# Level scores of two branches in three groups of two on TensorE, with VectorE's order changed to match

## The chip, the cores and the metric

One core of a Trainium2 chip runs the whole kernel. The metric is device time in microseconds, the median of the runs. PE is TensorE, DVE is VectorE, ACT is ScalarE, POOL is GpSimd, SP is SyncE, whose queue brings in the weights.

## The reference, cut to what matters

A decoder trunk of two layers: 512 tokens, width 1024. Each layer has a mixer of four parallel branches (mLSTM, GLA, S5, HGRN2), a cross-attention and an MLP. The change touches the two branches that use this function (GLA with 4 heads of 32 keys, HGRN with 4 heads of 64), in chunks of 64 tokens:

```python
def step(s_st, inp):
    qb, kb, vb, gb = inp
    g_end = gb[:, :, -1, :]
    o_inter = jnp.einsum('bhtk,bhkv->bhtv', qb * jnp.exp(gb), s_st)
    diff = gb[:, :, :, None, :] - gb[:, :, None, :, :]
    decay = jnp.exp(jnp.where(causal[:, :, None], diff, -jnp.inf))
    att = jnp.einsum('bhtk,bhsk,bhtsk->bhts', qb, kb, decay)
    o = o_inter + jnp.einsum('bhts,bhsv->bhtv', att, vb)
    s_new = (jnp.exp(g_end)[..., None] * s_st
             + jnp.einsum('bhsk,bhsv->bhkv', kb * jnp.exp(g_end[:, :, None, :] - gb), vb))
    return s_new, o
```

The branch outputs are normalised, gated, projected by `w_branch`, multiplied by sigmoid gates of the input (`gate` columns of `w_in`), summed, and projected by `w_out`.

## The kernel before

**Every engine has a list of its own, written out by hand.** Each runs its list in order; semaphores tie them. A wait at the head of an engine's list holds back all that stands behind it.

**Big matmuls.** Each weight matrix comes in blocks of 256 columns. A block (`gemm("m_o")`, `gate_parts(3, 1)`, `branch_gemm(3, 0)`) is cut into units of 256 rows: SP loads a unit, ACT writes its rounded part (`feed`, L1391), POOL the remainder, and PE does 12 matmuls of 128x128 by 512 for a unit (three products of split numbers, `parts`). A block of full depth has 4 units, a branch block 1. `some(block, n)` runs n units of a block and `rest(block)` what is left, so that other work can be put between. Blocks use two pairs of PSUM banks by turns; a block can start when the one before the last has been read out: of a gate block by ACT's tanh, of a branch block by DVE's `merge(n, c)` (L1982), which multiplies it by the gate and adds it up.

**Levels.** Within a chunk, the scores are split into seven levels: level 0 is the diagonal, and level l = 1 to 6 holds pairs of blocks of 32, 16, 8, 4, 2 and 1 tokens. For a branch m (`hg` or `gl`) and a level l:
- DVE `level_diff(m, l)` (L2002) writes the differences of the log decays to `m.E[l % 2]`; for l of 3 or more it needs level_mul l - 2.
- ACT `level_exp(m, l)` (L1510) takes the exponential in place.
- DVE `level_mul(m, l)` (L2014) multiplies keys and queries by it, into buffers that also go by l % 2; it needs the exponential, and for l of 3 or more that PE has done the scores of l - 2. It raises `x_ready`.
- PE `scores(m, l)` (L825, `pair_scores` L804): 32 small matmuls into the `mix` banks, when level_mul l is done and the bank is free. For HGRN, level l needs pick l - 4; for GLA, pick l - 2.
- DVE `pick(m, l)` (L2032) copies the valid scores from the bank into the score matrix under a mask.

Then DVE `last_decay` and `decayed` (L2056, L2063) make the decayed keys, with ACT's exponentials (`decays`, L1514) between them; PE `decayed_keys` (L853) transposes them, for which `decayed` and the picks that read the same banks must be done (HGRN pick 4, GLA pick 5); ACT copies them out; PE `state_in` (L862) needs pick 6 as well; DVE `states` adds up the chunk states and PE does `outputs`.

**ACT's list in the GLA part** is: exponential of level 1, copies of `m_v` (when PE has done that block), exponential of level 2 (L1676), copies of `m_o`, exponentials of levels 3 to 6, gate 3_1, `decays(gl)`, three tanhs for the mLSTM convolution, gate 3_2. The change leaves ACT's list as it is.

**Before the change** PE does the scores of levels 1 to 6 one by one, with 24 (HGRN) or 36 (GLA) big matmuls between two levels, and DVE picks each level as it comes.

Of the kernel before, what the change touches and what calls it, by code (L numbers as in the profile page):

```python
# [209 lines left out]
def build(nc, ins, out):  # L210
# [7 lines left out]
    with ctx:  # L218
# [59 lines left out]
        def of_layer(s, count):  # L278
            return s, count + now[0] * PER_LAYER[s.name]
# [211 lines left out]
        block = ctx.enter_context(nc.Block())  # L491
# [189 lines left out]
        def _(pe):  # L681
# [98 lines left out]
            def some(block, n):  # L780
                for _ in range(n):
                    next(block)

            def rest(block):
                for _ in block:
                    pass
# [38 lines left out]
            def scores(m, l):  # L825

                if l == 0:
                    pe.wait_ge(*of_layer(m.kq_ready, 3 - m.J))
                    if m.J == 2:
                        pe.wait_ge(*of_layer(m.g_ready, 5))  # L830
                    else:
                        pe.wait_ge(*of_layer(head_rs, 4))
                else:
                    pe.wait_ge(*of_layer(m.x_ready, l))
                if l >= 1:
                    pair_scores(m, l)
                    return
                kk, qq = (m.K, m.Q) if l == 0 else (m.X[l % 2], m.X[l % 2])

                n = CH if l == 0 else CH // 2  # L840
                for h in range(4):
                    rows = slice(m.dk * (h % m.per), m.dk * (h % m.per) + m.dk)
                    base = (h // m.per) * SEQ
                    for c in range(NCH):
                        at_ = m.score_cols(h) + (c // 2) * CH
                        tok = slice(base + c * CH, base + c * CH + CH)
                        late = qq[rows, tok]
                        if l:
                            late = late.rearrange("p (n a c) -> p n a c", a=2, c=LEVELS[l])[:, :, 1, :]
                        i = mm(m.score_bank(l, h)[64 * (c % 2):64 * (c % 2) + 64, at_:at_ + n], kk[rows, tok], late)  # L850
                i.then_inc(m.lev_done, 1)
# [104 lines left out]
            for L in range(DEPTH):  # L956
# [42 lines left out]
                    pe.wait_ge(p_vec, 10)  # L999
                mm(M[2][:, :], WA2[:, :], NT).then_inc(narrow_pe, 1)  # L1000
                rest(block)
                pe.wait_ge(*of_layer(gl.gate_in, 2))
                scores(hg, 1)
                block = parts("r_g", *H)
                some(block, 2)
                scores(hg, 2)
                rest(block)
                scores(hg, 3)
                block = gate_parts(3, 0)
                some(block, 2)  # L1010
                scores(hg, 4)
                rest(block)
                scores(hg, 5)
                block = parts("m_q", *H)
                some(block, 2)
                scores(hg, 6)
                some(block, 1)
                decayed_keys(hg)
# [9 lines left out]
                some(block, 1)  # L1028
                scores(gl, 0)
                rest(block)  # L1030
                scores(gl, 1)
                block = parts("m_o", *H)
                some(block, 3)
                scores(gl, 2)
                rest(block)
                branch_gemm(3, 0)
                scores(gl, 3)
                block = gate_parts(3, 1)
                some(block, 3)
                scores(gl, 4)  # L1040
                rest(block)
                branch_gemm(3, 1)
                block = gate_parts(3, 2)
                some(block, 1)
                scores(gl, 5)
                rest(block)
                scores(gl, 6)
                branch_gemm(3, 2)
                block = gate_parts(3, 3)
# [882 lines left out]
        def _(dve):  # L1932
# [81 lines left out]
            def level_mul(m, l):  # L2014
                w = LEVELS[l]
                dve.wait_ge(*of_layer(m.e_ready, l))
                if l >= 3:
                    dve.wait_ge(*of_layer(m.lev_done, l - 1))
                v = lambda ap: ap.rearrange("p (n a c) -> p n a c", a=2, c=w)
                e, xx, k, q = v(m.E[l % 2]), v(m.X[l % 2]), v(m.K), v(m.Q)  # L2020
                keys = KEYS[m.J][l % 2]
                if l <= (1, 2)[m.J - 1]:
                    tt(keys, m.E[l % 2], m.K, ALU.mult)
                else:
                    tt(v(keys)[:, :, 0, :], e[:, :, 0, :], k[:, :, 0, :], ALU.mult)
                of_chunk = lambda ap: ap.rearrange("p (n s) c -> p n s c", s=CH // (2 * w))
                late = m.X[l % 2].rearrange("p (n h s c) -> p n h s c", h=2, s=CH // (2 * w), c=w)
                for h in range(2):
                    own = const("in_pair")[:, 2 * m.J - 2 + h:2 * m.J - 1 + h]
                    stt(late[:, :, h, :, :], of_chunk(e[:, :, 1, :]), own, of_chunk(q[:, :, 1, :]), ALU.mult, ALU.mult, m.x_ready if h else None)  # L2030
# [96 lines left out]
            for L in range(DEPTH):  # L2127
# [71 lines left out]
                dve.wait_ge(*of_layer(gl.gate_in, 3))  # L2199
                stt(R(30)[:, 0, :], R(30)[:, 0, :], 0.0, R(31)[:, 0, :], ALU.min, ALU.subtract)  # L2200
                do(dve.tensor_tensor_scan(gl.Gc, reset, R(30)[:, 0, :], 0.0, ALU.mult, ALU.add))
                pick(hg, 1)
                level_diff(hg, 4)
                gate_out("g_r", gl.GR)
                level_mul(hg, 3)
                pick(hg, 2)
                level_diff(hg, 5)
                level_mul(hg, 4)
                pick(hg, 3)
                level_diff(hg, 6)  # L2210
                gate_out("r_g", hg.GR)
                level_mul(hg, 5)
                pick(hg, 4)
                level_mul(hg, 6)
                last_decay(hg)
                pick(hg, 5)
                decayed(hg)
                pick(hg, 6)
                decayed_queries(hg)
                states(hg)  # L2220
# [34 lines left out]
                do(dve.memset(CIN[:, :, 0:3], 0.0))  # L2255
                do(dve.memset(MONES, 1.0))
                level_mul(gl, 1)
                pick(gl, 0)
                level_diff(gl, 3)
                pick(gl, 1)  # L2260
                do(dve.tensor_copy(pr(17), Ur[:, S5_T, :]))
                do(dve.tensor_copy(pr(18), Ui[:, S5_T, :]))
                tt(Ur[:, :, :], Ur[:, :, :], PS[:, 8:8 + S5_T + 1, :], ALU.mult)
                tt(Ui[:, :, :], Ui[:, :, :], PS[:, 8:8 + S5_T + 1, :], ALU.mult)
                level_mul(gl, 2)
                level_diff(gl, 4)
                pick(gl, 2)
                tt(pr(5), re_, re_, ALU.mult)
                tt(pr(6), im_, im_, ALU.mult)
                tt(pr(5), pr(5), pr(6), ALU.add)  # L2270
# [9 lines left out]
                tt(pr(19), pr(19), pr(5), ALU.mult)  # L2280
                level_mul(gl, 3)
                level_mul(gl, 4)
                level_diff(gl, 5)
                level_diff(gl, 6)
                pick(gl, 3)
                merge(3, 0)
                conv(0)
                conv(1)
                pick(gl, 4)
                level_mul(gl, 5)  # L2290
                level_mul(gl, 6)

                def silu_of(j):
                    dve.wait_ge(*of_layer(ms["mth_ready"], j + 1))
# [1 line left out]

                last_decay(gl)
                conv(2)
                pick(gl, 5)
                decayed(gl)  # L2300
                merge(3, 1)
                conv(3)
                silu_of(0)
                silu_of(1)
                pick(gl, 6)
                decayed_queries(gl)
                merge(3, 2)
# [476 lines left out]
```

## Time and profile before

| what | us |
|---|---|
| median of 3 runs | 1968.84 (1968.78 to 1968.87) |
| the profiled execution | 1968.68 |
| its span, first to last instruction | 1966.8 |
| PE busy | 1936.9 (98%) |
| DVE busy | 1252.5 (64%) |
| POOL busy | 1134.1 (58%) |
| ACT busy | 966.5 (49%) |
| mean granted TensorE clock | 0.998 |

How to read it: the profile is of one execution. A row of the timeline gives the start and the length of a run of like instructions, the engine, the line, the operation, what is written and read with its shape, the count, and in brackets the idle time before it with what ended it. Most DVE rows carry the lines of two helpers (L1935, L1944), so they are told apart by shape, order and time. Times in the tables are from the start of the span. Layer 0's HGRN levels run from 93 to 130 us and its GLA levels from 157 to 214; layer 1's are 966 us later.

### The profile page before, as it was taken

How to read it: one execution, taken by the hardware profiler on the slowest of the kernel's cores; microseconds unless marked ns; L12 is line 12 of the kernel's file. 1: busy time of each engine (PE TensorE's matmuls, PEld its weight loads, DVE VectorE, ACT ScalarE, POOL GpSimd, SP SyncE). 2: the span in 40 equal slices, each digit the busy share in tenths (PEclk: the TensorE clock that was granted, in tenths of full speed). 3: DMA queues.
4: the chain of work that ended last, by engine and by line, in shares of the span. 5: the costliest groups of instructions: out<-in, count | busy, mean ns of one | idle time of the engine just before them, and what ended most of it. 6: DMA issues, size and time to landing. Idle time of an engine off the chain costs nothing.

```text
span 1966.8 us, 33324 instructions
## 1 busy us (share of the span) xinstructions
PE 1936.9 (98%) x12723; PEld 1642.3 (84%) x12723; DVE 1252.5 (64%) x1914; ACT 966.5 (49%) x1664; POOL 1134.1 (58%) x1356
## 2 busy tenths in 40 slices
PE   7999999999999999999999999999999999999998
PEld 6788788888888788989887877888898878989887
DVE  5887778856145766667358787787631566676662
ACT  6754545345445644344455546353553555444334
POOL 5565554946834556656564555368585446556653
PEclk9999999999999999999999999999999999999999
DMA  6423333333422333333333233233343233333331
GB/s 184 114 76 82 82 83 89 86 108 108 145 88 79 90 101 102 101 99 99 100 98 81 71 86 82 76 90 87 114 139 111 71 91 97 103 97 102 97 102 70
DMA packets 197275, 190.89 MB, mean 97 GB/s; under 512 B 23738, under 2 KB 190204, under 8 KB 196732
## 3 DMA queue, kind: packets, MB, share of 16 engines
q1 hardware_dynamic: 196252, 186.66, 32.5%
q8 instruction: 101, 1.65, 0.3%
q10 hardware_dynamic: 864, 2.10, 0.3%
q14 instruction: 58, 0.48, 0.1%
HBM read 184.51 MB, written 3.15 MB: 95 GB/s over the span
## 4 chain that ended last, share of the span: by engine, by line
PE 89%; DVE 6%; ACT 3%; issue 1%; DMA 1%; DVEq 0%; POOL 0%; SPq 0%; ACTq 0%
PE gemm L683 69%; PE mix L683 18%; DVE work L1935 1%; DVE h_lo L1944 1%; ACT w_hi L1401 1%; DVE sums_raw L1935 1%; DVE work_split L1944 1%; DVE x_t L1935 0%; DMA w_raw<-in_mlp_w_dram 0%; DVE work L1944 0%; PE mix L1265 0%; DMA work<-in_norm_mix_dram 0%; DVE gate_t L1944 0%; DVE w_raw L1935 0%; ACT work_split L1569 0%
## 5 line engine op out<-in xcount | busy, mean ns | idle before, releaser
L676 POOL TENSOR_TENSOR w_lo<-w_raw,w_hi 128x256 fp32r<-128x256 f32 x676 | 590.8, 874 | 804.6 <-ACT w_hi L1401 804.6
L677 POOL TENSOR_TENSOR w_lo<-w_raw,w_hi 128x256 fp32r<-128x256 f32 x676 | 594.6, 880 | 0.0
L683 PE MATMUL gemm<-h_hi,w_hi 128*128 128x512 f32 x1312 | 519.4, 396 | 3.6 <-DVE h_lo L1944 2.1
L683 PE MATMUL gemm<-h_lo,w_hi 128*128 128x512 f32 x1312 | 511.2, 390 | 0.0
L683 PE MATMUL gemm<-h_hi,w_lo 128*128 128x512 f32 x1312 | 511.1, 390 | 0.0
L683 PE MATMUL gemm<-work_split,w_hi 128*128 128x512 f32 (+1 forms) x1552 | 447.4, 373 | 2.7 <-ACTq L1507 1.4
L1401 ACT ACTIVATE w_hi<-w_raw 128x512 fp32r<-128x512 f32 x676 | 378.2, 621 | 53.3 <-DMA w_raw<-in_w_in_dram 24.7
L683 PEld LDWEIGHTS gemm<-work_split,w_hi 128*128 128x128 f32 x1552 | 281.2, 188 | 54.4 <-DVE work_split L1944 2.6
L683 PEld LDWEIGHTS gemm<-h_hi,w_hi 128*128 128x128 f32 x1312 | 246.3, 188 | 64.7 <-issue 8.8
L683 PEld LDWEIGHTS gemm<-h_hi,w_lo 128*128 128x128 f32 x1312 | 246.3, 188 | 52.0
L683 PE MATMUL gemm<-work_split,w_lo 128*128 128x512 f32 (+1 forms) x776 | 288.5, 372 | 0.0
L683 PEld LDWEIGHTS gemm<-h_lo,w_hi 128*128 128x128 f32 x1312 | 246.4, 188 | 49.7 <-issue 1.0
L683 PEld LDWEIGHTS gemm<-work_split,w_lo 128*128 128x128 f32 x776 | 146.2, 188 | 25.5
L1935 DVE TENSOR_TENSOR x_t<-x_t,gemm 128x512 f32<-128x512 f32 x96 | 66.0, 688 | 119.8 <-PE gemm L683 114.7
L1399 ACT ACTIVATE gate_rows<-sums_raw 128x768 fp32r<-128x768 f32 x48 | 40.6, 846 | 201.8 <-DVE sums_raw L1935 201.8
L1935 DVE TENSOR_TENSOR work<-work 128x512 f32<-128x512 f32 (+5 forms) x142 | 125.0, 880 | 14.3 <-ACT work L1612 6.5
L683 PE MATMUL mix<-work_split,w_hi 128*128 128x256 f32 (+1 forms) x544 | 121.0, 286 | 0.1
L1506 ACT ACTIVATE gate_t<-gemm 128x512 f32<-128x512 f32 x52 | 31.1, 599 | 141.0 <-PE gemm L683 140.5
L683 PE MATMUL mix<-work_split,gate_rows 128*128 128x256 f32 x456 | 97.8, 283 | 0.0
L683 PEld LDWEIGHTS mix<-work_split,w_hi 128*128 128x128 f32 x544 | 91.9, 191 | 3.2 <-issue 0.8
L683 PEld LDWEIGHTS mix<-work 64*64 64x64 f32 (+4 forms) x3136 | 76.9, 129 | 17.7 <-issue 14.4
L1935 DVE TENSOR_TENSOR sums_raw<-w_raw 128x256 f32<-128x256 f32 (+1 forms) x53 | 31.9, 601 | 84.5 <-DMA w_raw<-in_mlp_w_dram 83.2
(363 smaller groups left out, 2742.1 us busy)
## 6 DMA issues: line engine op xcount, KB each, us to landing
w_raw<-in_mlp_w_dram SPq DMA_DIRECT2D x256, 256.0 KB, 2.7
w_raw<-in_w_in_dram SPq DMA_DIRECT2D x208, 256.0 KB, 2.7
w_raw<-in_xattn_w_kv_dram SPq DMA_DIRECT2D x64, 256.0 KB, 3.0
w_raw<-in_w_branch_dram SPq DMA_DIRECT2D x32, 256.0 KB, 2.7
w_raw<-in_w_out_dram SPq DMA_DIRECT2D x32, 256.0 KB, 2.7
w_raw<-in_xattn_w_q_dram SPq DMA_DIRECT2D x32, 256.0 KB, 2.8
w_raw<-in_xattn_w_o_dram SPq DMA_DIRECT2D x32, 256.0 KB, 2.7
w_raw<-in_w_in_dram SPq DMA_DIRECT2D x32, 128.0 KB, 3.4
```

The costliest lines, as they stand in the source:

```text
L676: pool.tensor_tensor(lo[:, 0:half], raw[:, 0:half], hi[:, 0:half].bitcast(F32), ALU.subtract)
L677: pool.tensor_tensor(lo[:, half:], raw[:, half:], hi[:, half:].bitcast(F32), ALU.subtract).then_inc(split_ready, 1)
L683: return pe.matmul(o, w, a, start=start, stop=stop, skip_group_check=True)
L1399: act.activation(SWhi[d // 2 % 2], SWraw[d // 2 % 2], ACT.Copy)
L1401: act.activation(hi, raw, ACT.Copy).then_inc(split_hi, 1)
L1506: do(act.activation(t[:, b, :], G[s][b][:, :], ACT.Tanh, scale=0.5), th_ready)
L1935: do(dve.tensor_tensor(o, a, b, op), s)
L1944: do(dve.scalar_tensor_tensor(out=o, in0=a, scalar=sc, in1=b, op0=op0, op1=op1), s)
```

## The change

On PE, the scores of levels 1 and 2, 3 and 4, 5 and 6 now stand side by side, for both branches, and the parts of big blocks that stood between them come before the pair. On DVE, the two `level_mul` of a pair are done one after the other, and then the two picks. In the GLA part `level_mul(gl, 2)` comes ahead of `pick(gl, 0)`; picks 1 and 2 go behind `level_mul(gl, 4)`; `decayed(gl)` and `pick(gl, 5)` go behind `merge(3, 1)` and `conv(3)`, and `pick(gl, 5)` also behind two `silu_of`. Nothing is added to or taken from any engine's list; what is computed is the same.

```diff
@@ -999,20 +999,20 @@
                     pe.wait_ge(p_vec, 10)
                 mm(M[2][:, :], WA2[:, :], NT).then_inc(narrow_pe, 1)
                 rest(block)
+                block = parts("r_g", *H)
+                some(block, 2)
                 pe.wait_ge(*of_layer(gl.gate_in, 2))
                 scores(hg, 1)
-                block = parts("r_g", *H)
-                some(block, 2)
                 scores(hg, 2)
                 rest(block)
-                scores(hg, 3)
                 block = gate_parts(3, 0)
                 some(block, 2)
+                scores(hg, 3)
                 scores(hg, 4)
                 rest(block)
-                scores(hg, 5)
                 block = parts("m_q", *H)
                 some(block, 2)
+                scores(hg, 5)
                 scores(hg, 6)
                 some(block, 1)
                 decayed_keys(hg)
@@ -1028,22 +1028,21 @@
                 some(block, 1)
                 scores(gl, 0)
                 rest(block)
-                scores(gl, 1)
                 block = parts("m_o", *H)
                 some(block, 3)
+                scores(gl, 1)
                 scores(gl, 2)
                 rest(block)
                 branch_gemm(3, 0)
-                scores(gl, 3)
                 block = gate_parts(3, 1)
                 some(block, 3)
+                scores(gl, 3)
                 scores(gl, 4)
                 rest(block)
                 branch_gemm(3, 1)
                 block = gate_parts(3, 2)
-                some(block, 1)
+                rest(block)
                 scores(gl, 5)
-                rest(block)
                 scores(gl, 6)
                 branch_gemm(3, 2)
                 block = gate_parts(3, 3)
@@ -2199,22 +2198,22 @@
                 dve.wait_ge(*of_layer(gl.gate_in, 3))
                 stt(R(30)[:, 0, :], R(30)[:, 0, :], 0.0, R(31)[:, 0, :], ALU.min, ALU.subtract)
                 do(dve.tensor_tensor_scan(gl.Gc, reset, R(30)[:, 0, :], 0.0, ALU.mult, ALU.add))
-                pick(hg, 1)
                 level_diff(hg, 4)
                 gate_out("g_r", gl.GR)
                 level_mul(hg, 3)
+                level_mul(hg, 4)
+                pick(hg, 1)
                 pick(hg, 2)
                 level_diff(hg, 5)
-                level_mul(hg, 4)
-                pick(hg, 3)
                 level_diff(hg, 6)
                 gate_out("r_g", hg.GR)
                 level_mul(hg, 5)
+                level_mul(hg, 6)
+                pick(hg, 3)
                 pick(hg, 4)
-                level_mul(hg, 6)
                 last_decay(hg)
+                decayed(hg)
                 pick(hg, 5)
-                decayed(hg)
                 pick(hg, 6)
                 decayed_queries(hg)
                 states(hg)
@@ -2255,16 +2254,14 @@
                 do(dve.memset(CIN[:, :, 0:3], 0.0))
                 do(dve.memset(MONES, 1.0))
                 level_mul(gl, 1)
+                level_mul(gl, 2)
                 pick(gl, 0)
                 level_diff(gl, 3)
-                pick(gl, 1)
+                level_diff(gl, 4)
                 do(dve.tensor_copy(pr(17), Ur[:, S5_T, :]))
                 do(dve.tensor_copy(pr(18), Ui[:, S5_T, :]))
                 tt(Ur[:, :, :], Ur[:, :, :], PS[:, 8:8 + S5_T + 1, :], ALU.mult)
                 tt(Ui[:, :, :], Ui[:, :, :], PS[:, 8:8 + S5_T + 1, :], ALU.mult)
-                level_mul(gl, 2)
-                level_diff(gl, 4)
-                pick(gl, 2)
                 tt(pr(5), re_, re_, ALU.mult)
                 tt(pr(6), im_, im_, ALU.mult)
                 tt(pr(5), pr(5), pr(6), ALU.add)
@@ -2280,15 +2277,17 @@
                 tt(pr(19), pr(19), pr(5), ALU.mult)
                 level_mul(gl, 3)
                 level_mul(gl, 4)
+                pick(gl, 1)
+                pick(gl, 2)
                 level_diff(gl, 5)
                 level_diff(gl, 6)
-                pick(gl, 3)
                 merge(3, 0)
                 conv(0)
                 conv(1)
-                pick(gl, 4)
                 level_mul(gl, 5)
                 level_mul(gl, 6)
+                pick(gl, 3)
+                pick(gl, 4)
 
                 def silu_of(j):
                     dve.wait_ge(*of_layer(ms["mth_ready"], j + 1))
@@ -2296,12 +2295,12 @@
 
                 last_decay(gl)
                 conv(2)
-                pick(gl, 5)
-                decayed(gl)
                 merge(3, 1)
                 conv(3)
+                decayed(gl)
                 silu_of(0)
                 silu_of(1)
+                pick(gl, 5)
                 pick(gl, 6)
                 decayed_queries(gl)
                 merge(3, 2)
```

## Rows read from the trace of the kernel before

**Rows 1.** The page: busy time by engine, and the chain's shares by engine.
```profile
PE 1936.9 (98%) x12723; PEld 1642.3 (84%) x12723; DVE 1252.5 (64%) x1914; ACT 966.5 (49%) x1664; POOL 1134.1 (58%) x1356
...
PE 89%; DVE 6%; ACT 3%; issue 1%; DMA 1%; DVEq 0%; POOL 0%; SPq 0%; ACTq 0%
```

**Rows 2.** The chain in order of time: start us, us, what.
```profile
1939.92 13.38 PE gemm L683 x59
```

**Rows 3.** Timeline of PE, HGRN levels 1 and 2 of layer 0.
```profile
92.90 1.15 PE L683 MATMUL mix<-work 128*64 128x64 f32 x32
...
99.65 1.15 PE L683 MATMUL mix<-work 128*64 128x64 f32 x32
```

**Rows 4.** Groups of PE by form: count | busy us, mean ns of one | idle.
```profile
L683 PE MATMUL mix<-work 128*64 128x64 f32 x384 | 13.8, 225 | 0.0
```

**Rows 5.** Timeline of PE: GLA levels 1 to 3, transposes, state_in.
```profile
164.32 0.69 PE L683 MATMUL mix<-work 64*64 64x64 f32 x32
...
173.33 0.69 PE L683 MATMUL mix<-work 64*64 64x64 f32 x32
...
179.97 0.69 PE L683 MATMUL mix<-work 64*64 64x64 f32 x32 [0.28 <-DVE work L1944]
...
210.54 0.60 PE L859 MATMUL mix<-consts_sb,work 128*128 128x128 f32 x4
...
214.06 1.42 PE L683 MATMUL mix<-work 64*32 64x64 f32 x64
```

**Rows 6.** Timeline of PE, HGRN outputs of layer 0.
```profile
141.48 2.79 PE L683 MATMUL mix<-work 64*64 64x64 f32 x120
```

**Rows 7.** Timeline of ACT: m_v's last copy, exponentials 2 and 3 of GLA.
```profile
164.43 0.60 ACT L1674 ACTIVATE work<-gemm 128x512 f32<-128x512 f32 x1 [0.84 <-PE gemm L683]
165.14 0.63 ACT L1512 ACTIVATE work<-work 128x512 f32<-128x512 f32 x1
...
177.73 1.30 ACT L1512 ACTIVATE work<-work 128x512 f32<-128x512 f32 x2
```

**Rows 8.** Timeline of DVE, GLA part of layer 0.
```profile
157.62 0.69 DVE L1935 TENSOR_TENSOR work<-work 128x512 f32<-128x512 f32 x1
...
160.11 1.91 DVE L2044 COPY_PREDICATED work<-masks_sb,mix 128x256 f32<-128x256 int32 x4
...
165.15 0.75 DVE L2054 COPY_PREDICATED work<-masks_sb,mix 128x512 f32<-128x512 int32 x1 [1.20 <-PE mix L683]
...
167.34 0.89 DVE L1935 TENSOR_TENSOR work<-work 128x256 f32<-128x256 f32 x1
...
174.16 0.72 DVE L2054 COPY_PREDICATED work<-masks_sb,mix 128x512 f32<-128x512 int32 x1 [2.42 <-PE mix L683]
...
178.45 0.43 DVE L1935 TENSOR_TENSOR work<-work 128x256 f32<-128x256 f32 x1 [0.91 <-ACT work L1512]
...
202.40 1.37 DVE L2054 COPY_PREDICATED work<-masks_sb,mix 128x512 f32<-128x512 int32 x1
...
212.58 1.37 DVE L2054 COPY_PREDICATED work<-masks_sb,mix 128x512 f32<-128x512 int32 x1
...
235.60 0.48 DVE L2324 MEMSET work<- 64x512 f32 x1 [5.25 <-ACT work L1704]
```

**Rows 9.** Timeline of DVE, layer 1: GLA level_mul 3.
```profile
1144.50 0.43 DVE L1935 TENSOR_TENSOR work<-work 128x256 f32<-128x256 f32 x1 [0.90 <-ACT work L1512]
```

**Rows 10.** Timeline of PE, start of the kernel.
```profile
7.14 3.62 PE L926 MATMUL mix<-consts_sb,work 128*128 128x128 f32 x16
...
15.98 1.03 PE L926 MATMUL mix<-consts_sb,work 128*128 128x128 f32 x8
...
24.97 0.47 PE L683 MATMUL gemm<-w_hi,work_split 128*128 128x512 f32 x1 [1.99 <-POOL w_lo L677]
25.28 0.40 PE L683 MATMUL gemm<-w_hi,merged_split 128*128 128x512 f32 x1
```

**Rows 11.** Stretches: PE, PEld, DVE, ACT, POOL busy, granted clock, DMA share, GB/s.
```profile
1960.00:1967.00 7.00, 0.00 (x0) 0.00 (x0) 1.73 (x3) 1.72 (x3) 0.00 (x0) 0.50 0.75 300
```

## The prediction

> **What bounds the kernel now.** I read the page first, for one question: which engine has no idle time. TensorE (PE) is busy 98% of the span and holds 89% of the chain that ended last, nearly all of it in the big matmuls of line 683 [rows 1]. So the time is the time in which PE gets through its own list, and an edit counts in two ways only: by what it takes off or puts on that list, and by waits that it makes or ends there. Next I read the timeline of PE around the level scores, to see what one group of them costs beyond its own matmuls; then ACT and DVE in the GLA stretch of layer 0, to see how early each group's inputs are ready. The numbers below are those of layer 0.
>
> **What a group of scores costs PE.** Over a long run big matmuls take a step of 0.227 us (13.38 us for 59) [rows 2]. One HGRN level is 32 small matmuls; 384 of them in the kernel are 2 layers of 6 levels. They take 1.15 us to the end of the last, one lasts 0.225, so the step is (1.15 - 0.225) / 31 = 0.030 and 32 are 0.96 us [rows 3, 4]. From the start of level 1 (92.90) to that of level 2 (99.65) are 6.75 us, and in them 32 small and 24 big matmuls: 0.96 + 24 x 0.227 = 6.41. So **one switch from big to small and back costs 0.34 us**. In GLA, level 1 to level 2 is 173.33 - 164.32 = 9.01 us for 32 small at (0.69 - 0.22) / 31 = 0.015 and 36 big: 0.49 + 8.17 = 8.66, leaving 0.35 us [rows 5]. Two lots of small matmuls back to back do not pay this: 120 of the HGRN outputs, with semaphore waits among them, run as one stretch of 2.79 us, 0.022 each [rows 6].
>
> The change makes 3 groups of 6 in each branch, so 3 switches fewer, 4 times over: 6 x 0.34 + 6 x 0.35 = **4.1 us off PE's list**, 2.07 per layer, nothing hiding it. The levels' own matmuls stay. The zero ends of the bound: if joining two levels did cost a switch, this gain would be nothing; the HGRN outputs are the nearest row, and I take the whole.
>
> **Two waits of PE that go.** GLA level 3 waited 0.28 us for DVE and started 0.35 late by the usual step; it now stands 36 big matmuls later, so this goes. GLA's state_in, at 214.06, started right behind pick 6 (213.95 [rows 5, 8]), some 0.2 late by the usual step; this too is overtaken by what follows.
>
> **HGRN: do the inputs come in time?** PE reaches the pairs at about 98.3, 111.5 and 124.6 us (92.9, then 24, 48 and 48 big matmuls, a switch and 2.0 us for each pair between). Levels 1 and 2 are multiplied long before. DVE has lost pick 1 (0.77 us) ahead of level_mul 3 and gained nothing there, so levels 3 and 4 are ready by about 109, and with some 3.4 us for each further level_mul levels 5 and 6 by about 122: 2 us to spare. decayed(hg) now stands right behind last_decay and waits for ACT's exponential, about 1.1 us, but ends near 127.9 where PE needs it at 129.5. So HGRN costs nothing and its 1.0 us per layer stands. If this cover were gone, each late us would be one us of PE.
>
> **GLA: where it goes wrong.** level_mul(gl, 2) is moved ahead of pick(gl, 0), next to level_mul 1. It needs ACT's exponential of level 2. That sits in ACT's list behind the copies of m_v, and those wait for PE to finish m_v: the last copy starts at 164.43, the exponential at 165.14 and ends at 165.8 [rows 7]. Before, DVE used that time: pick 0 at 160.11, level_diff 3, and pick 1 at 165.15 [rows 8]. After, PE is 1.03 us ahead, so the exponential ends at 164.8, while DVE is at level_mul 2 already at 160.11 - 1.03 = 159.1. **DVE stands still for 5.7 us**, with pick 0, level_diff 3 and 4 and the S5 arithmetic queued behind it.
>
> DVE then has this to do until level_mul 3: before, from 157.62 to 178.45 are 20.8 us, less the idle 1.20 + 2.42 + 0.91 = 16.3 of work [rows 8]; less level_mul 1 (157.62 to 160.11, 2.5) and picks 1 and 2 (1.5, now later) are 12.3. 164.8 + 12.3 = 177.1. The exponential of level 3 is ready at about the same time: PE ends m_o 1.4 us earlier than before (1.03 and one switch), so 177.73 + 0.66 - 1.4 = 177.0 [rows 7]. level_mul 3 thus starts at **177.1, 1.35 earlier** than the 178.45 of before.
>
> From there DVE has no idle time left: before, 178.45 to the end of pick 6 at 212.58 + 1.37 = 213.95 [rows 8] is 35.5 us of steady work. After, the two picks of 0.75 us (1.5 with their gaps) have been added to it, and pick 5, which stood at 202.40 ahead of decayed, merge(3, 1) and conv 3, now stands behind these and behind two silu steps, next to last. Its end: 177.1 + 35.5 + 1.5 - 1.4 (pick 6) = 212.7. Durations are not fixed: the same form, a 128x256 product, took 0.89 us at 167.34 and 0.43 at 178.45 [rows 8], and level_mul 5 and decayed move into other company. From 0.4 us less to 1.2 more; I take 0.6 more: **pick 5 ends at 213.3.**
>
> PE needs pick 5 for decayed_keys(gl), whose transposes write the banks that it reads. Before, pick 5 was done at 203.8 and PE came at 210.54 [rows 5, 8]: 6.8 us to spare. After, PE comes at 210.54 - 2.07 (six switches) - 0.35 (the wait at level 3) = 208.1 and waits until 213.4, **5.3 us idle**. Queued behind it are the transposes, gate3_3, state_in and all that follows; ACT's feed of weights is ahead and does not matter. The other gates on the way hold: levels 3 and 4 at 186.4 (177.1 + two level_muls, 3.0, + two picks, 1.5 = 181.6), levels 5 and 6 at 204.0 (picks 3 and 4 by 199.3, summed the same way along DVE's list), branch3_2's bank at 205.2 (merge(3, 1) by 204.7, thin).
>
> decayed_keys to state_in was 3.52 us with the wait of 0.2, so 3.3: state_in starts at 216.7 instead of 214.06, **2.65 us late per layer, 5.3 in all**. Later steps of DVE and ACT hang on PE's results (DVE idles 5.25 us ahead of 235.60 [rows 8]), so nothing gives this back. Layer 1 repeats layer 0 some 966 us later: the idle time ahead of level_mul 3, 0.91 us here, is 0.90 there [rows 8, 9].
>
> **The clock on top.** The longest idle time of PE between its first matmul and its last is 1.99 us, early in layer 0. Where it had stood idle, at the start, 16 transposes took 3.62 us; the same form ran 8 in 1.03 us nine us later [rows 10], that is 0.22 and 0.11 us each: the lower level (1.2 GHz) against the upper (2.4 GHz). At the end, with PE idle, the granted clock reads 0.50 [rows 11]. A wait of 5.3 us is more like these two than like the short ones. If the clock falls, matmuls take twice the step for a while: 3.62 us in which 1.75 us of work are done cost 1.87 us. Bounds 0 and 1.9 per layer; I take 1.5, near that row, since part of the slow stretch may fall into the wait. That is 3.0 us.
>
> The Trainium skill, page "TensorE: Matmul & The Clock Gate", section Part 1, says that an array left idle goes to half clock and gets it back only after sustained work. It speaks against this change, as the grouping saves 0.35 us a time and the wait can cost the clock; by it the sum holds the 3.0, without it 5.3 stands alone. No stretch of this trace has such an idle time in mid-run.
>
> **Sum.** 5.3 + 3.0 = +8.3 us. The profiled execution took 1968.68 us (span 1966.8), the median is 1968.84; on the median **1977.1 us**. Some 0.2% (3.9 us) either way is what a measurement can tell from no change.
>
> **Rivals.**
> 1. The wait comes, the clock holds (or falls in one layer): 1968.84 + 5.3 = 1974.1, or 1975.6. For it: the big matmuls right behind the idle 1.99 us took 0.47 and 0.40 us, the usual [rows 10]. Chance 0.32.
> 2. The wait is about half as long, because DVE's forms run at their shorter durations and picks are quick: break-even is a wait of 2.07 + 0.35 + 0.2 = 2.6 us, that is pick 5 by about 210.7. Time 1966 to 1972.5. Against: the steady 35.5 us is a sum of measured rows. Chance 0.13.
> 3. The other side, faster: DVE keeps up and the switches alone count. It decides at pick 5 ending by 208.1, so DVE would have to find 5 us, for instance if the exponential of level 2 did not come behind m_v. Then 1968.84 - 4.1 - 0.7 - 0.4 = 1963.6. Chance 0.07.
> 4. A second wait: merge(3, 1) late for branch3_2, or the HGRN pairs late, 1 us or more per layer: 1979.5 and over. Chance 0.06.
>
> The forecast has 0.42. **Range** 1972.0 to 1979.5: from the wait at its short bound with no fall of the clock to both at their long one. The likeliest case's own range is 1974.9 to 1979.5. Faster by over 0.2%: 0.07 (rival 3). Within: rival 2 and the short edge of 1, 0.14. Slower: 0.79.
>
> **What would show it.** In the trace of after: PE's level groups of 64 small matmuls, each pair followed by big ones, the first at 98.3; DVE idle ahead of level_mul(gl, 2) for 5 to 6 us, released by ACT; level_mul(gl, 3) at about 177; the second half of pairs 5-6 at 205; PE idle ahead of the 4 transposes of line 859 for about 5 us, released by DVE, in both layers; granted clock under 1.00 just behind. Wrong would be: DVE idle short at level_mul 2, PE idle under 2.6 us, or a clock at 1.00 throughout.

## The result and the profile after

| what | before | after |
|---|---|---|
| median of 6 runs each, us | 1968.72 (1968.48 to 1968.87) | 1978.81 (1977.98 to 1979.82) |
| the profiled execution | 1968.68 | 1978.68 |
| its span | 1966.8 | 1976.9 |

The change makes the kernel slower: 1.0052 times the time before (95% interval 1.0041 to 1.0062), 10.1 us. The forecast was 1977.1 in a range of 1972.0 to 1979.5.

The page of after, busy time by engine and the chain's shares by engine:

```profile
PE 1937.0 (98%) x12723; PEld 1646.4 (83%) x12723; DVE 1246.3 (63%) x1914; ACT 966.1 (49%) x1664; POOL 1130.0 (57%) x1356
...
PE 85%; DVE 10%; ACT 3%; issue 1%; DMA 1%; DVEq 0%; POOL 0%; SPq 0%; ACTq 0%
```

PE does the same work in the same busy time, and its share of the chain has gone from 89% to 85%, DVE's from 6% to 10% [rows 1]. So the end is now set by DVE in some place where it was PE before. The timeline of PE in after says where. First, HGRN in layer 0:

```profile
78.91 1.56 PE L683 MATMUL mix<-work 64*64 64x64 f32 x64
...
99.01 2.09 PE L683 MATMUL mix<-work 128*64 128x64 f32 x64
...
112.13 2.09 PE L683 MATMUL mix<-work 128*64 128x64 f32 x64
```

In before the level 0 scores stood here:

```profile
78.24 1.56 PE L683 MATMUL mix<-work 64*64 64x64 f32 x64
```

The profiled execution of after is thus 0.67 us late already ahead of the first thing that was changed. It comes from the start: PE's first matmul is at 7.52 against 6.87, both waiting for the same DMA, and other executions have it anywhere from 6.6 to 7.9. It is taken off below wherever a time of after stands against one of before. With it taken off, the first pair is at 98.34. The pairs have no wait, and one cycle of a pair and 48 big matmuls is 112.13 - 99.01 = 13.12 us, where two levels and 48 big matmuls took 2 x 6.75 = 13.50 [rows 3]. One switch is 0.38 us.

Then GLA, same view:

```profile
204.62 1.16 PE L683 MATMUL mix<-work 64*64 64x64 f32 x64
...
214.76 1.09 PE L859 MATMUL mix<-consts_sb,work 128*128 128x128 f32 x4 [6.03 <-DVE work L2053]
215.50 0.78 PE L683 MATMUL gemm<-h_hi,w_hi 128*128 128x512 f32 x1
...
217.87 0.39 PE L683 MATMUL gemm<-h_hi,w_hi 128*128 128x512 f32 x1
...
219.33 1.42 PE L683 MATMUL mix<-work 64*32 64x64 f32 x64
...
1185.17 1.09 PE L859 MATMUL mix<-consts_sb,work 128*128 128x128 f32 x4 [6.03 <-DVE work L2053]
...
1190.86 1.42 PE L683 MATMUL mix<-work 64*32 64x64 f32 x64
```

The switch costs the same here. Over two levels and 72 big matmuls, from level 4 to level 6 in before (189.02 to 207.05, 18.03 us) and from the second pair to the third in after (186.98 to 204.62, 17.64), the timelines differ by 0.39 us. Between levels 2 and 3 of GLA stood 24 big matmuls in before, not the 36 of the other gaps.

PE is ready for the transposes at 208.7, idles 6.03 us until pick 5 has ended on DVE (line 2053), and starts them at 214.76. It does so in both layers. Behind the idle time the transposes take 1.09 us for 4, where they took 0.60 [rows 5], and the first big matmul 0.78 where the later ones take 0.39. The stretches of after say the same in the granted clock (PE, PEld, DVE, ACT, POOL busy, granted clock, DMA share, GB/s):

```profile
213.00:215.00 2.00, 0.24 (x2) 0.27 (x3) 1.93 (x3) 0.00 (x0) 0.83 (x1) 0.76 0.00 0
215.00:219.40 4.40, 4.40 (x18) 3.41 (x19) 3.06 (x4) 3.31 (x6) 2.12 (x4) 0.72 0.00 0
...
1184.00:1186.00 2.00, 0.83 (x5) 0.86 (x5) 1.97 (x2) 0.00 (x0) 0.24 (x1) 0.50 0.00 0
1186.00:1190.80 4.80, 4.80 (x14) 3.56 (x12) 2.46 (x4) 3.31 (x6) 3.11 (x5) 0.56 0.02 5
```

TensorE works at the lower of its two levels (1.2 GHz) for part of the stretch in layer 0 and for most of it in layer 1. The Trainium skill, page "TensorE: Matmul & The Clock Gate", section Part 1, says that an array left idle goes to half clock until it has been busy for a while; these rows agree, with 0.50 to 0.76 behind 6.03 us of idle time.

**Where the 10.1 us are.** From transposes to state_in are 219.33 - 214.76 = 4.57 us in layer 0 and 1190.86 - 1185.17 = 5.69 in layer 1. At full clock it is 3.30 (`e_two_units` below: 214.30 to 217.61). So the clock costs 1.27 + 2.39 = 3.7 us. state_in is 219.33 - 0.67 - 214.06 = 4.60 us late in layer 0 [rows 5], of which 4.60 - 1.27 = 3.33 are lateness at full clock: the wait less what the grouping saved. In layer 1 of before it stood here:

```profile
1180.08 1.42 PE L683 MATMUL mix<-work 64*32 64x64 f32 x64 [0.17 <-issue]
```

That is 10.78 us later in after; less 0.67 and 4.60, layer 1 adds 5.51, of which 2.39 are the clock and 3.12 the lateness. The two spans differ by 10.1 and not by 10.8, so some 0.7 us, the size of the late start, come back behind that.

DVE in the same stretch of after, layer 0 (timeline):

```profile
165.43 0.42 DVE L1934 TENSOR_TENSOR work<-work 128x256 f32<-128x256 f32 x1 [5.82 <-ACT work L1511]
...
177.64 0.43 DVE L1934 TENSOR_TENSOR work<-work 128x256 f32<-128x256 f32 x1 [1.25 <-ACT work L1511]
...
194.25 0.85 DVE L1934 TENSOR_TENSOR work<-work 128x256 f32<-128x256 f32 x1
195.13 1.72 DVE L1943 SCALAR_TENSOR_TENSOR work<-work,consts_sb 128x256 f32<-128x256 f32 x2
196.89 0.85 DVE L1934 TENSOR_TENSOR work<-work 128x256 f32<-128x256 f32 x1
...
209.89 1.10 DVE L1934 TENSOR_TENSOR work<-work 128x512 f32<-128x512 f32 x1
211.02 2.22 DVE L1943 SCALAR_TENSOR_TENSOR work<-work 128x512 f32<-128x512 f32 x2
213.28 2.72 DVE L2053 COPY_PREDICATED work<-masks_sb,mix 128x512 f32<-128x512 int32 x2
```

DVE stands 5.82 us ahead of level_mul 2 and 1.25 more ahead of level_mul 3, both for ACT's exponentials (line 1511), and from there it is busy until pick 5 ends in the middle of the last row, at about 214.6.

### The profile page after: what moved, and what is told of

It reads as the page before. It is cut to its first block, busy times and chain, and to the rows that moved or that the text cites. A ratio compares the mean times of both kernels' runs of the same rounds, so it can differ in the third digit from the quotient of the medians.

```text
span 1976.9 us, 33324 instructions
## 1 busy us (share of the span) xinstructions
PE 1937.0 (98%) x12723; PEld 1646.4 (83%) x12723; DVE 1246.3 (63%) x1914; ACT 966.1 (49%) x1664; POOL 1130.0 (57%) x1356
## 4 chain that ended last, share of the span: by engine, by line
PE 85%; DVE 10%; ACT 3%; issue 1%; DMA 1%; DVEq 0%; POOL 0%; SPq 0%; ACTq 0%
PE gemm L683 66%; PE mix L683 18%; DVE work L1943 2%; DVE work L1934 2%; DVE h_lo L1943 1%; ACT w_hi L1400 1%; DVE sums_raw L1934 1%; DVE work_split L1943 1%; DVE work L2053 0%; DVE x_t L1934 0%; DMA w_raw<-in_mlp_w_dram 0%; PE mix L1264 0%; DVE work L1940 0%; DVE merged L1943 0%; DMA work<-in_norm_mix_dram 0%
## 5 line engine op out<-in xcount | busy, mean ns | idle before, releaser
L1934 DVE TENSOR_TENSOR sums_raw<-w_raw 128x256 f32<-128x256 f32 (+1 forms) x53 | 27.5, 519 | 86.4 <-DMA w_raw<-in_mlp_w_dram 85.0
```

Source lines behind the costliest of these rows:

```text
L1934: do(dve.tensor_tensor(o, a, b, op), s)
```

## The experiments

Every kernel below is after with one edit, unless it says before. Times are medians; the kernel before took 1968.6 to 1968.9 beside them.

**1. Which half costs?** Two kernels with the change in one branch only. `e_hg_only` has the HGRN hunks of the diff and leaves GLA as in before:

```
+                block = parts("r_g", *H)
+                some(block, 2)
                 pe.wait_ge(*of_layer(gl.gate_in, 2))
                 scores(hg, 1)
-                block = parts("r_g", *H)
-                some(block, 2)
                 scores(hg, 2)
...
-                pick(hg, 1)
...
                 level_mul(hg, 3)
+                level_mul(hg, 4)
+                pick(hg, 1)
                 pick(hg, 2)
```

> The HGRN half of the change alone, on PE and DVE; the GLA part as before. Theory (each switch between small and big matmuls costs PE 0.34 to 0.38 us and HGRN has slack): 6 switches fewer, 2.0 to 2.3 us less than before, about 1966.5; PE never idle in the HGRN part. Rival (the pairs cost as much as they save, or delay weights and gates): no change, 1968.7.

Measured: 1966.64 us, 0.9989 (0.9981 to 0.9998), 2.2 us faster. PE has no wait in HGRN. The six switches give 6 x 0.38 = 2.3 us and nothing takes them back.

`e_gl_only` has the GLA hunks and leaves HGRN as in before:

```
-                scores(gl, 1)
                 block = parts("m_o", *H)
                 some(block, 3)
+                scores(gl, 1)
                 scores(gl, 2)
...
                 level_mul(gl, 1)
+                level_mul(gl, 2)
                 pick(gl, 0)
...
-                pick(gl, 5)
-                decayed(gl)
                 merge(3, 1)
                 conv(3)
+                decayed(gl)
                 silu_of(0)
                 silu_of(1)
+                pick(gl, 5)
```

> The GLA half alone, on PE and DVE; the HGRN part as before. Theory (all of the loss lies in GLA, at the transposes that wait for pick 5): the HGRN gain of 2.2 us is missing, so about 1981, with PE idle some 6 us ahead of the four transposes of each layer. Were part of the loss in HGRN, it would be below 1978.8.

Measured: 1982.59, 1.0070 (1.0056 to 1.0083), 13.7 us slower. PE idles 6.02 and 6.04 us ahead of the transposes. Its layer 0:

```profile
215.93 1.09 PE L859 MATMUL mix<-consts_sb,work 128*128 128x128 f32 x4 [6.02 <-DVE work L2053]
```

```profile
216.00:221.00 5.00, 5.00 (x15) 4.09 (x16) 3.23 (x4) 3.31 (x6) 2.55 (x4) 0.52 0.00 0
```

After plus the lost 2.2 us of HGRN would be 1981.0. Of the other 1.6, the trace puts 1.0 on the clock, which is at the lower level in nearly all of the stretch in both layers here (0.52 and 0.51): from transposes to state_in are 5.60 and 5.65 us, against 4.57 and 5.69 in after. The rest is open. The whole loss is in GLA. The idle time is the same as in after, though PE comes 1.2 us later: exponential 3 stands behind m_o, so it comes later with PE too (178.10 against 176.92 in ACT's timeline), and DVE with it.

**2. What makes DVE late: the exponential of level 2?** It stands behind m_v's copies in ACT's list. `e_exp2_early` puts it ahead of them:

```
                 level_exp(gl, 1)
+                level_exp(gl, 2)
                 for b, bank, free in banks("m_v"):
...
-                level_exp(gl, 2)
                 for b, bank, free in banks("m_o"):
```

> The changed kernel, with ACT's exponential of GLA level 2 moved ahead of the copies of m_v. Theory A (the prediction's chain: DVE stands 5.8 us for this exponential, and that makes pick 5 late): DVE gains about 5 us from there, pick 5 is done in time, and the time falls to about 1966 to 1969. Theory B (the exponential of level 3, behind the copies of m_o, holds level_mul 3 just as long): DVE's wait only moves from level_mul 2 to level_mul 3, which starts at 177 to 177.6 as now; time unchanged, 1978 to 1980.

Measured: 1980.97, 1.0060 (1.0046 to 1.0073). That is no faster than after but 2.2 us slower, and 1.0 above what Theory B allowed. The profiled execution is the fastest of the four (1978.76, the others 1980.7 to 1981.7), so what adds the 2.2 us is in no trace. DVE in its timeline, level_mul 2 first and then level_mul 3:

```profile
158.82 0.85 DVE L1934 TENSOR_TENSOR work<-work 128x256 f32<-128x256 f32 x1
...
177.14 0.43 DVE L1934 TENSOR_TENSOR work<-work 128x256 f32<-128x256 f32 x1 [4.08 <-ACT work L1511]
```

The wait at level_mul 2 is gone, and DVE waits 4.08 us at level_mul 3 in place of it. PE's idle time is 6.02 us again. So the 5.8 us at level_mul 2, the most striking idle time of DVE in the trace of after, cost nothing by themselves: the exponential of level 3, behind m_o's copies, sets the same start.

**3. Both exponentials.** `e_exps_early` puts levels 3 and 4 ahead of m_o's copies as well:

```
-                level_exp(gl, 2)
+                level_exp(gl, 3)
+                level_exp(gl, 4)
                 for b, bank, free in banks("m_o"):
...
-                level_exp(gl, 3)
-                level_exp(gl, 4)
                 level_exp(gl, 5)
```

> The changed kernel, with ACT's exponential 2 ahead of the copies of m_v and exponentials 3 and 4 ahead of the copies of m_o. Theory B: now level_mul 3 is held by PE's scores of level 1 (about 172.7), 4 to 5 us earlier; pick 5 ends about 4.5 us earlier, PE waits 1 to 2 us instead of 6 and its clock stays up: about 1979 - 9 - 3.7 = 1966 to 1968. If DVE's steady work between level_mul 3 and pick 5 stretches (weights being split beside it), 1970 to 1972.

Measured: 1968.41, 0.9995 (0.9986 to 1.0004), no difference from before, and 0.4 above the 1966 to 1968 of Theory B. The profiled execution is the slowest of ten, 1972.03. Level_mul 3 and the transposes of both layers:

```profile
173.72 0.42 DVE L1934 TENSOR_TENSOR work<-work 128x256 f32<-128x256 f32 x1
```

```profile
210.82 0.63 PE L859 MATMUL mix<-consts_sb,work 128*128 128x128 f32 x4 [1.99 <-DVE work L2053]
...
1177.62 0.63 PE L859 MATMUL mix<-consts_sb,work 128*128 128x128 f32 x4 [1.93 <-DVE work L2053]
```

level_mul 3 starts 3.9 us earlier than in after and PE's idle time is 4.0 us shorter. DVE's chain from level_mul 3 to pick 5 to the transposes is thus rigid, one us for one us. level_mul 3 could have come earlier still, but DVE's small S5 steps ahead of it took longer; the last section shows why.

**4. Is it pick 5's place alone?** `e_late_pick5` is before, with the last picks in the order of after and no pairs:

```
-                pick(gl, 5)
-                decayed(gl)
                 merge(3, 1)
                 conv(3)
+                decayed(gl)
                 silu_of(0)
                 silu_of(1)
+                pick(gl, 5)
                 pick(gl, 6)
```

> The kernel before, with one move of the change alone: on DVE, pick 5 and the decayed keys of GLA go behind merge(3,1), conv 3 and two silu steps. Theory (the move of pick 5 is harmful by itself): pick 5 ends at about 212.6 instead of 203.8, PE comes to the transposes at 210.5 and waits 2.1 us, state_in starts near 216.0 instead of 214.1: 1.9 us per layer, 1972.5 us in all, up to 2 us more where the clock falls. Rival (only the pairing does harm, since pick 5 had 6.8 us to spare): 1968.7.

Measured: 1975.81, 1.0036 (1.0022 to 1.0050), 7.2 us slower than before.

```profile
213.04 0.63 PE L859 MATMUL mix<-consts_sb,work 128*128 128x128 f32 x4 [2.56 <-DVE work L2054]
```

```profile
213.40:217.90 4.50, 4.50 (x15) 3.35 (x13) 2.95 (x4) 3.31 (x6) 2.80 (x5) 0.62 0.00 0
```

In layer 1 the wait is 2.57 us and the clock behind it 0.63. Two waits of 2.56 us, less the 0.2 each that state_in no longer waits, are 4.7 us of the 7.2; the rest goes to the clock. The profiled execution is the slowest of the four (1977.98). In it, from transposes to state_in are 4.89 and 4.91 us instead of 3.30, so 3.2 us for two falls, and the clock falls a third time behind an idle 1.82 us at 1626.86. How many falls the faster executions have, no trace shows. The single number of the expectation, which left the clock out, is missed by 3.3 us; with up to 2 us for the fall in each layer (1976.5) the time fits. Pick 5's place alone, without any pairs, makes PE wait.

`e_picks_early` does the opposite: it is after, with pick 5, decayed and pick 6 of GLA right behind merge(3, 1), and ACT's copy of the transposed keys one step forward:

```
                         gate(3, 2)
+                        kt_copy(gl)
...
-                kt_copy(gl)
...
                 merge(3, 1)
-                conv(3)
+                pick(gl, 5)
                 decayed(gl)
+                pick(gl, 6)
+                conv(3)
                 silu_of(0)
                 silu_of(1)
-                pick(gl, 5)
-                pick(gl, 6)
```

> The changed kernel, with pick 5, the decayed keys and pick 6 on DVE right behind merge(3,1), ahead of conv 3 and the silu steps, and on ACT the copy of the transposed keys ahead of the last tanh of the convolution, which waits for conv 3. Theory (it is the place of pick 5, not the start of DVE's work, that decides): pick 5 ends at about 207.2, before PE comes at 208.7, no wait at the transposes or at state_in: 1968.7 - 4.5 - 0.7 - 0.4 = 1963.1. Rival: the later conv 3 and silu steps make a new wait at the outputs or in the mLSTM part, 1965 or more.

Measured: 1963.17, 0.9972 (0.9962 to 0.9982), 5.4 us faster than before.

```profile
207.59 0.60 PE L859 MATMUL mix<-consts_sb,work 128*128 128x128 f32 x4
```

```profile
204.74 1.37 DVE L2053 COPY_PREDICATED work<-masks_sb,mix 128x512 f32<-128x512 int32 x1
206.15 0.96 DVE L1934 TENSOR_TENSOR work<-work 128x512 f32<-128x512 f32 x1
```

Pick 5 ends at 206.1 and decayed at 207.1, and PE goes into the transposes with no wait, although both waits of DVE for exponentials are still there. The pairs are sound; the loss is the conv step and the silus that stand ahead of a pick that PE waits for. The 5.4 us are the twelve switches, 12 x 0.38 = 4.6, and the waits that go at level 3 (0.28 us [rows 5]) and at state_in (some 0.2) in each layer.

`e_picks_exps` joins this with the edit of 3.

> e_picks_early with the early exponentials of e_exps_early as well. Theory (PE has no wait left in this stretch): the same time as e_picks_early, 1963.2, within 0.5. Rival (DVE's earlier start takes away a wait later on, in the mLSTM part): 1 us or more less.

Measured: 1963.03, 0.9971 (0.9960 to 0.9982): the same. Once pick 5 is in time, earlier exponentials are worth nothing.

**5. Cover for the wait.** PE has big matmuls of gate3_3 behind the transposes, and they need nothing from DVE. `e_one_unit` and `e_two_units` put one or two units of them ahead:

```
                 block = gate_parts(3, 3)
+                some(block, 1)
                 decayed_keys(gl)
```

(`some(block, 2)` in the second.)

> The changed kernel, with one of the four units of gate3_3 (12 big matmuls, 2.7 us) ahead of the transposes that wait for pick 5. Theory (PE's idle time is loss, the wait itself stays where it is): idle 3.3 us instead of 6.0, so 5.4 us less in all; 1973.4 if the clock still falls as in the changed kernel, about 1970 if it holds.

Measured: 1974.94, 1.0028 (1.0019 to 1.0038); single runs from 1971.37 to 1976.15. The profiled one is the fastest of them:

```profile
214.41 0.68 PE L859 MATMUL mix<-consts_sb,work 128*128 128x128 f32 x4 [3.38 <-DVE work L2054]
```

```profile
214.40:218.40 4.00, 3.99 (x13) 3.23 (x14) 3.32 (x4) 3.18 (x6) 1.88 (x3) 0.57 0.00 0
1182.60:1185.90 3.30, 3.27 (x16) 2.57 (x16) 3.02 (x4) 2.51 (x5) 1.20 (x2) 1.00 0.02 5
```

The idle time is 3.38 us in layer 0 and 3.36 in layer 1; the clock fell in the first and held in the second. The median is 1.5 us above the higher of the two numbers expected: the expectation had the clock cost at most what it cost in after, and most executions lie above that. That one kernel spreads over 4.8 us fits with falls that come in some executions and not in others, here or elsewhere in the kernel (the last section has such falls behind idle times of 1.8 us); only one of them has a trace, so this is argued and not shown.

> The changed kernel, with two units of gate3_3 (24 big matmuls, 5.5 us) ahead of the transposes. Theory: PE waits about 0.5 us, the clock holds; what is left is the gain of the pairs, 12 switches by 0.37 and the old waits at level 3: 1968.7 - 4.5 - 0.7 + 0.5 = 1964. Rival (pick 5 late is also late for what follows: state_in, the chunk states, the outputs): 1967 or more.

Measured: 1964.77, 0.9983 (0.9974 to 0.9992), 3.8 us faster than before.

```profile
214.30 0.63 PE L859 MATMUL mix<-consts_sb,work 128*128 128x128 f32 x4 [0.68 <-DVE work L2054]
...
217.61 1.42 PE L683 MATMUL mix<-work 64*32 64x64 f32 x64
```

Two units are 24 x 0.227 = 5.4 us of cover for 6.03 of wait, and 0.68 are left. DVE is as late as in after; it is the idle time of PE, not DVE's lateness, that costs.

**6. The clock by itself.** `e_dummy` is after with 24 useless big matmuls ahead of the transposes. They write a bank that the next block overwrites, so PE is as late as in after but not idle:

```
                 block = gate_parts(3, 3)
+                s, used = psum_set("gate3_3")
+                pe.wait_ge(gemm_free[s][0], used)
+                for _ in range(24):
+                    mm(G[s][0][:, :], Hhi[:, 0, 0:P], Hhi[:, 1, :])
                 decayed_keys(gl)
```

> The changed kernel, with 24 big matmuls of no use (5.4 us, their result is overwritten) ahead of the transposes that wait for pick 5; all waits stay where they are. Theory (the clock's fall is a loss of its own, on top of the wait): PE has no long idle time left there, the clock stays up, the transposes start at the same time (214.8), the steps behind them are short again: 1978.8 less 1.3 us in layer 0 and 2.4 us in layer 1, 1975.1. Rival (the slow steps behind the wait have another cause, such as weights not ready): 1978.8.

Measured: 1975.77, 1.0035 (1.0022 to 1.0047), 7.2 us slower than before and 3.0 less than after. Its transposes, and the stretch behind them:

```profile
213.90 0.63 PE L859 MATMUL mix<-consts_sb,work 128*128 128x128 f32 x4 [0.68 <-DVE work L2057]
```

```profile
214.00:219.00 5.00, 5.00 (x82) 4.08 (x83) 3.49 (x6) 3.31 (x6) 3.04 (x5) 1.00 0.10 21
```

This execution began 0.95 us earlier than that of after (level 0 of HGRN at 77.96 against 78.91), so the transposes are as late as there: 214.85 against 214.76. The granted clock is 1.00 here and from 1185 to 1190 in layer 1. So of the 10.1 us, 7.2 are lateness and about 3 the lower clock: matmuls that compute nothing of use make the kernel 3 us faster.

**7. Pairs on PE, DVE as before.** `e_pe_only` takes all DVE hunks of the diff back and keeps those of PE. Of its edit, the part around level_mul 2:

```
                 level_mul(gl, 1)
-                level_mul(gl, 2)
                 pick(gl, 0)
                 level_diff(gl, 3)
-                level_diff(gl, 4)
+                pick(gl, 1)
...
+                level_mul(gl, 2)
+                level_diff(gl, 4)
+                pick(gl, 2)
```

> The pairs on PE alone; DVE's order as before. Theory: DVE picks level 1 ahead of level_mul 2, 3, ..., so the second level of a pair must wait. In HGRN picks 3 and 5 stand ahead of level_mul 5 and 6 and the like, and PE waits at levels 4 and 6 for pick, level_diff, exponential and level_mul, 2 to 5 us each; in GLA likewise at level 2 (pick 1, then 1.4 + 2.7 us: about 4 us). Together 5 to 12 us per layer: 1980 to 1995. Rival (DVE's order hardly matters): below 1970.

Measured: 1985.39, 1.0084 (1.0070 to 1.0098), the slowest of all.

```profile
176.99 1.13 PE L683 MATMUL mix<-work 64*64 64x64 f32 x32 [3.29 <-DVE work L1943]
...
214.72 1.22 PE L683 MATMUL gemm<-work_split,w_hi 128*128 128x512 f32 x2 [3.06 <-DVEq L1991]
```

PE waits 3.29 us in the middle of the first GLA pair for level_mul 2, and 3.06 for a branch bank that DVE has not yet read out; the clock falls at both (0.60 and 0.59). In layer 1 they are 3.29 and 3.02. The time lies in the expected range, but its two halves do not both hold: in HGRN, where 2 to 5 us were expected at levels 4 and at 6, PE waits once for 0.42 us in a layer, and the wait for the branch bank was not expected. Ahead of the transposes PE does not wait. Moving level_mul 2 ahead of pick 1 was needed for the pairs. Moving pick 5 behind conv 3 and the silus was not.

## Why the prediction was right in kind and 1.7 us short

**The switch** was a little under-sized: 0.34 to 0.35 us forecast, 0.38 by the cycle of 13.12 us, which is 4.6 us and not 4.1 for the twelve. The prediction built a cycle up from single steps, one of them worked out of the end of a run of small matmuls; two whole cycles set against each other need no such step. That HGRN has no wait held (first pair 98.3 forecast, 98.34 measured; `e_hg_only` -2.2 us).

**PE's arrival** at the transposes was forecast at 208.1 and came at 214.76 - 6.03 - 0.67 = 208.06.

**DVE's stand at level_mul 2** was forecast at 5.7 us and was 5.82; level_mul 3 at 177.1, measured 177.64 - 0.67 = 176.97. Here the numbers were right, the second partly by luck, and part of the reading was wrong. The 177.1 was summed along DVE's list (12.3 us from level_mul 2 on); DVE got through that list in 11.0 us and stood ready at 175.7. What held the start at 177 was ACT's exponential of level 3, which the prediction had at 177.0 and did not take for the binding one. The step says that the exponential of level 3 "is ready at about the same time", but rival 3 then lets DVE find its 5 us "if the exponential of level 2 did not come behind m_v". `e_exp2_early` refutes that: with it early, the wait moves to level 3 and nothing is gained. Two chains ended together, and both had to be moved (`e_exps_early`).

**Pick 5's end** is the step that was mis-sized: 213.3 forecast, 214.64 - 0.67 = 213.97 measured, 0.07 beyond the upper bound given. The term is the 0.6 us for durations in other company. Level_mul 5 and 6 took 0.85 + 1.72 + 0.85 + 1.01 = 4.43 us; in before they were 0.80 + 1.36 + 0.43 + 1.01 = 3.60. decayed took 1.10 against 0.69. In before (timeline of DVE):

```profile
194.99 0.80 DVE L1935 TENSOR_TENSOR work<-work 128x256 f32<-128x256 f32 x1
195.83 1.36 DVE L1944 SCALAR_TENSOR_TENSOR work<-work,consts_sb 128x256 f32<-128x256 f32 x2
197.22 0.43 DVE L1935 TENSOR_TENSOR work<-work 128x256 f32<-128x256 f32 x1
...
203.80 0.69 DVE L1935 TENSOR_TENSOR work<-work 128x512 f32<-128x512 f32 x1
```

That is 1.24 us where 0.6 stood. PE's idle time was therefore 6.03 us and not 5.3, and the lateness without the clock 3.33 us in layer 0 instead of 2.65.

**The clock** fell in both layers, for 1.27 and 2.39 us, 3.7 together, and 3.0 by `e_dummy`; forecast 3.0. Layer 1's 2.39 lies above the bound of 1.9 that was read from the start of the kernel: 16 transposes at half speed are not the longest slow stretch that there can be. Rival 1 (the clock holds) did not come true; `e_dummy` is that rival as a kernel, and measured 1975.8 where the rival gave 1974.1; pick 5's lateness of 0.7 us a layer is most of the difference.

**The sum**: 8.3 forecast, 10.1 measured. Lateness at full clock is 3.33 + 3.12 = 6.45 where 5.3 stood, 1.15 more, and the clock 3.66 where 3.0 stood, 0.66 more: the missing 1.8. The dearer switch is no part of it. The four switches of a layer that stand ahead of exponential 3 bring DVE forward with PE, as `e_gl_only` shows (without the three of HGRN, the transposes start 1.2 us later, with the same idle time); the two behind it only make PE wait longer. Neither makes the kernel slower.

**The other rivals.** 2, the wait half as long: not in after, but `e_exps_early`, with 1.99 us, came out at 1968.4, inside its 1966 to 1972.5. 3, faster: `e_picks_early` is this case by another way, 1963.2 against its 1963.6. 4, a second wait: none in after; `e_pe_only` has it.

## What to carry to other kernels

Where one engine sets the time, find for each of its steps the operation of another engine that it waits for, and put that operation as early in that engine's list as its own inputs allow; a conv or silu that nobody waits for goes behind it. Count an idle time of TensorE at more than its length, since the clock may fall with it, and have independent matmuls ready to stand ahead of the wait (two units turned +10.1 us into -3.8). The longest idle time of a helper engine isn't by itself the cause: ask what it would wait for next.

## What the runs showed of the hardware

**The clock can fall behind short idle times, and need not behind longer ones.** The granted clock fell behind 2.56 us (`e_late_pick5`, both layers) and 1.93 us (`e_exps_early`, layer 1), and held behind 1.99 us in layer 0 of the same execution and behind 3.36 us in `e_one_unit`. It also falls far from the change: PE idles 1.8 us once in each layer (at 652.96 and 1619.02 in before, for DVE), with a clock of 1.00 behind it in before and after, and 0.57 behind 1.83 us in `e_exps_early`. Stretches of that execution, behind 1.99, 1.83 and 1.93 us of idle time:

```profile
210.80:214.10 3.30, 3.28 (x16) 2.55 (x16) 3.02 (x4) 2.53 (x5) 1.22 (x2) 1.00 0.03 9
652.90:656.50 3.60, 3.50 (x7) 2.25 (x8) 3.41 (x6) 2.99 (x4) 3.60 (x5) 0.57 0.10 34
1177.60:1182.50 4.90, 4.88 (x16) 3.51 (x16) 3.34 (x4) 3.31 (x6) 2.82 (x5) 0.65 0.07 22
```

The same 16 matmuls take 3.3 us in the first and 4.9 in the last. Between about 1.8 and 3.4 us of idle time both outcomes occur in these traces; behind 6.0 it fell all six times (after, `e_gl_only` and `e_exp2_early`, both layers). What decides between the two is left open.

**DVE and POOL slow each other.** In after, DVE did small S5 steps while POOL had nothing to do; in `e_exps_early` the same steps came earlier, beside POOL's remainders of the weights. After first, then `e_exps_early`, DVE and then POOL:

```profile
174.82 0.17 DVE L1934 TENSOR_TENSOR s_small<-s_small,params_all 128x8 f32<-128x8 f32 x1
```

```profile
168.66 0.66 DVE L1934 TENSOR_TENSOR s_small<-s_small,params_all 128x8 f32<-128x8 f32 x1
169.36 0.66 DVE L1934 TENSOR_TENSOR s_small<-s_pw,params_all 128x8 f32<-128x8 f32 x1
```

```profile
168.56 0.74 POOL L677 TENSOR_TENSOR w_lo<-w_raw,w_hi 128x256 fp32r<-128x256 f32 x1
169.26 0.74 POOL L676 TENSOR_TENSOR w_lo<-w_raw,w_hi 128x256 fp32r<-128x256 f32 x1
```

A product of 8 elements a partition takes 0.66 us instead of 0.17, and one starts 0.1 us after each of POOL's starts: the two step together. The Trainium skill, page "SBUF — State Buffer", section "SBUF: two separate sides", says that a VectorE operation with two SBUF inputs and a GpSimd operation that reads SBUF take a shared port in turns, each for a whole instruction; these rows agree. It is also the likely cause of the 0.43 and 0.85 us for the same 128x256 product, and so of the term that was mis-sized. The picks, which read one operand from PSUM, do not stretch: in before, pick 5 at 202.40 with POOL idle and pick 6 at 212.58 beside two of POOL's subtractions took 1.37 us each.
